# Spreading a head pair's two reciprocal sums over columns: one DVE copy of a broadcast view in place of two ACT operations

## The reference

```python
score = einsum('bqh,bqhs->bqs', wb, relu(einsum('bqhd,bsd->bqhs', qib, k_idx)))
_, idx = lax.top_k(where(causal, score, -inf), 256)      # the keys each query may see
att = einsum('bqhd,bqkd->bhqk', qb, k[idx]) * HEAD_DIM ** -0.5 - slopes * dist
p = jax.nn.softmax(att, axis=-1)                         # 8 query heads, one key/value head
y = einsum('bhqk,bqkd->bqhd', p, v[idx])                 # HEAD_DIM = 64
```

## Time and profile before

| | |
|---|---|
| median of 3 runs | 3352.51 us (3343.8 to 3353.59) |
| the profiled execution, its own time | 3356.66 us |
| its span | 3354.5 us |
| PE busy | 3200.5 us, 95% |
| DVE busy | 2065.4 us, 62% |
| ACT busy | 1310.3 us, 39% |
| POOL busy | 743.8 us, 22% |
| mean granted clock of TensorE | 0.981 of full speed |

### The profile page before, as it was taken

How to read it: one execution, slowest core, us unless ns; L and a number is a source line. 1 busy time by engine, 2 the same in 40 slices (tenths; PEclk the granted TensorE clock), 3 DMA queues, 4 the chain that set the end, 5 groups by cost and what they waited for, 6 DMA issues and landing times.

```text
span 3354.5 us, 41929 instructions
## 1 busy us (share of the span) xinstructions
PE 3200.5 (95%) x15077; PEld 2640.3 (79%) x15077; DVE 2065.4 (62%) x3529; ACT 1310.3 (39%) x2277; POOL 743.8 (22%) x546
## 2 busy tenths in 40 slices
PE   8987999999999999999999999999899998989998
PEld 7865788788888788778887778876788887778886
DVE  5997457688808448598994853759868288610001
ACT  4336421533238431441113843137773177421111
POOL 3431200065774000011322400000211323001212
PEclk9998999999999999999999999999999999999999
DMA  7973756599992656535554055652455510445554
GB/s 228 304 239 122 290 191 207 182 288 291 289 297 108 245 202 218 182 145 195 190 199 145 20 220 203 219 199 81 163 191 198 195 51 20 171 150 193 196 189 169
DMA packets 178528, 635.97 MB, mean 190 GB/s; under 512 B 11357, under 2 KB 96905, under 8 KB 116776
## 3 DMA queue, kind: packets, MB, share of 16 engines
q1 hardware_dynamic: 163728, 582.00, 50.2%
q10 hardware_dynamic: 14616, 51.47, 3.9%
HBM read 474.04 MB, written 159.38 MB: 189 GB/s over the span
## 4 chain that ended last, share of the span: by engine, by line
PE 75%; DVE 7%; ACT 4%; issue 4%; DMA 1%; POOL 0%; ACTq 0%; DVEq 0%; POOLq 0%; SPq 0%
PE PS L1763 19%; PE PS L1725 14%; PE PS L1727 14%; PE PS L1726 14%; PE PS L1930 3%; PE PS L1748 1%; PE PS L1749 1%; PE PS L1750 1%; DVE probs L1593 1%; PE PS L1949 1%; PE PS L1950 1%; PE PS L1809 1%; ACT TMP L838 1%; ACT probs L958 1%; PE PS L1977 1%
## 5 line engine op out<-in xcount | busy, mean ns | idle before, releaser
L1763 PE MATMUL PS<-WS,HT 128*128 128x512 f32 x2088 | 484.3, 392 | 16.1 <-ACT TMP L1082 10.4
L1763 PEld LDWEIGHTS PS<-WS,HT 128*128 128x128 f32 x2088 | 394.5, 189 | 99.7 <-ACT TMP L1082 10.8
L553 POOL TENSOR_TENSOR WS<-RAW,WS 128x1024 fp32r<-128x1024 f32 x116 | 281.1, 2424 | 577.5 <-ACT WS L709 562.2
L1725 PE MATMUL PS<-HF,WS 128*128 128x512 f32 x1024 | 400.5, 391 | 6.9 <-DVE HF L1171 4.6
L637 POOL TENSOR_TENSOR TMP<-TMP 128x512 f32<-128x512 f32 x88 | 113.6, 1291 | 1316.2 <-ACT TMP L1082 1316.2
L1726 PE MATMUL PS<-HF,WS 128*128 128x512 f32 x1024 | 400.1, 391 | 0.0
L1727 PE MATMUL PS<-HF,WS 128*128 128x512 f32 x1024 | 400.0, 391 | 0.0
L1351 DVE TENSOR_SCALAR_CACHE_REDUCE flags<-W,cand 128x640 uint8<-128x640 f32 (+9 forms) x272 | 372.6, 1370 | 35.6 <-DVE cand L1386 27.8
L1725 PE MATMUL PS<-HT,WS 128*128 128x512 f32 x816 | 322.2, 395 | 0.8 <-POOL WS L553 0.6
L1727 PE MATMUL PS<-HT,WS 128*128 128x512 f32 x816 | 317.7, 389 | 0.0
L1726 PE MATMUL PS<-HT,WS 128*128 128x512 f32 x816 | 317.6, 389 | 0.0
(11 more groups left out here) (283 smaller groups left out, 6490.0 us busy)
## 6 DMA issues: line engine op xcount, KB each, us to landing
WS<-split_weights_scratch SPq DMA_DIRECT2D x234, 1024.0 KB, 4.8
split_weights_scratch<-WS SPq DMA_DIRECT2D x116, 1024.0 KB, 5.0
W<-split_weights_scratch SPq DMA_DIRECT2D x114, 1024.0 KB, 4.8
RAW<-in_w_in SPq DMA_DIRECT2D x34, 512.0 KB, 6.0
RAW<-in_w_ffn_gate SPq DMA_DIRECT2D x22, 512.0 KB, 6.3
RAW<-in_w_ffn_up SPq DMA_DIRECT2D x22, 512.0 KB, 6.4
RAW<-in_w_ffn_down SPq DMA_DIRECT2D x22, 512.0 KB, 5.7
gate_b_scratch<-TMP ACTq DMA_DIRECT2D x32, 256.0 KB, 5.3
```

What stands on the lines that cost most here:

```text
L553: nc.gpsimd.tensor_tensor(out=WS[:, slot, 1, :], in0=RAW[:, slot, :], in1=WS[:, slot, 0, :].bitcast(f32), op=ALU.subtract).then_inc(w_lo, 1)
L1725: mm(PS[:, bank, :], wh, src[:, 0, k, :], start=k == 0, stop=False)
L1763: ins = mm(PS[:, 2 * t + half, :], lhs, split(c, w_part)[:, half * 512:(half + 1) * 512], start=first and part == 0 and w_part == 0, stop= ...
```

## The change

DVE takes over the spreading. Behind its reciprocal it waits for its own result and copies a broadcast view of `rs` (each of the two values read 64 times) to the 128 columns of `rsb`, in one operation. ACT's `spread_sums` and its two calls are gone, and so is the tile `ones`, with the memset of POOL that filled it at the start. DVE's wait ahead of the reciprocal is now for `pv_psum` (PE has read the place of `rsb` that is to be written) and no longer for ACT's spreading of two pairs before; PE waits for one count of `rsb_ready` a pair instead of two, and, from the third pair on, also for `bc_done` of two pairs before.

```diff
-                    def spread_sums(n):
-                        act.wait_ge(recip_done, n + 1)
-                        if n >= 2:
-                            act.wait_ge(pv_psum, n - 1)
-                        for f in range(2):
-                            nc.scalar.activation(rsb[:, n % 2, DH * f:DH * f + DH], ones[:, :], ACT.Copy,
-                                                 scale=rs[:, n % 2, f:f + 1]).then_inc(rsb_ready, 1)
...
-                                if e == 1 and u == 0:
-                                    spread_sums(PAIRS * g + i - lag)
...
-                            if i >= lag and e == 1 and not banks:
-                                spread_sums(PAIRS * g + i - lag)
...
                                     if n >= 2:
-                                        dve.wait_ge(rsb_ready, 2 * n - 2)
+                                        dve.wait_ge(pv_psum, n - 1)
...
                                     nc.vector.reciprocal(rs[:, n % 2, :], total).then_inc(recip_done, 1)
+                                    dve.wait_ge(recip_done, n + 1)
+                                    nc.vector.tensor_copy(rsb[:, n % 2, :].rearrange("p (f d) -> p f d", f=2),
+                                                          rs[:, n % 2, :].rearrange("p (f o) -> p f o", o=1).to_broadcast([P, 2, DH])).then_inc(rsb_ready, 1)
...
-                            pe.wait_ge(rsb_ready, 2 * n + 2)
+                            pe.wait_ge(rsb_ready, n + 1)
+                            if n >= 2:
+                                pe.wait_ge(bc_done, n - 1)
```

More of the change, by code:

```diff
@@ L240, in build_block @@
         meanm = sb("meanm", [P, P], f32)
-        ones = sb("ones", [P, DH], f32)
         upper = sb("upper", [P, P], f32)
@@ L563, in _ @@
             nc.gpsimd.memset(meanm[:, :], 1.0 / CC)
-            nc.gpsimd.memset(ones[:, :], 1.0)
             chained(nc.gpsimd.memset(upper[:, :], 0.0))
```

## The result

The changed kernel takes 3364.11 us (median of 5 runs, 3361.67 to 3369.03), the kernel before beside it 3352.14 (median of 5). By these medians it is 12.0 us slower. The recorded ratio, which is not that of the two medians (1.0036), is 1.0048 with a 95% interval of 1.0036 to 1.0059, that is 16 us, 12 to 20. Forecast were 3369.1 us and +14.5. Of the 5.0 us between forecast and median, 2.5 are the size of the change, the rest is the base I counted from (3354.6 against 3352.14). One of the 11 executions of the version in which POOL's product waits for the copy took 12777 us at a mean granted clock of 0.55, and its ratio is of the ten others.

What follows compares the result with a forecast made beforehand. Mostly TensorE bounds the kernel, but in attention groups 0 and 2 a loop of engine waits. Groups 0 to 3 added 6.4, 2.0, 4.4 and 1.7 us, together 14.5, on 3354.6: 3369.1 us, range 3354 to 3389.

Steps and rivals of the forecast that it cites:

- What bounds the loop: Attention groups 0 and 2: engines wait in a loop, and DVE's part from reciprocal to exponential lies on it; turn 3.44 us.
- The step of one copy: Behind DVE's reciprocal: 0.26 us a pair, 0.49 where POOL's product holds the copy in group 0, 0.28 in group 2.
- Rival 3: All groups: copy takes one column a cycle and doesn't meet POOL; step 0.34 us, 13.2 us in all, 3367.8 us; chance 8%.
- Group 0: First attention stage: 13 pairs at 0.49 us, 2 at 0.26, less half a microsecond: +6.4 us.
- ACT's relief: ACT's two spreading operations gone: nothing in groups 0 and 2, -1.5 us in group 1, -1.4 in group 3.
- Group 1: Second attention stage, PE full: copies 1.3 us, a meeting with POOL 2.2, less 1.5 for ACT: +2.0 us.
- the meeting with POOL's 2.40 us product: Group 1, one pair: POOL's product with the gain begins just ahead of the copy and holds it, 2.2 us.
- Group 2: Third attention stage: 16 pairs at a step of 0.28 us make 4.5, of which 4.4 us were taken.
- Group 3: Fourth attention stage: step on the loop at 12 of 16 pairs, 3.1 us, less 1.4 for ACT: +1.7 us.
- the copy that was to find POOL idle: Group 3, four pairs: POOL's product already holds DVE's sum, so the copy behind it meets no POOL work.
- rival 1: POOL's scaling by a scalar per partition holds the copy too, mainly four pairs of group 3; 28 us, 3382.6 us; chance 33%.
- Rival 4: Group 2: POOL's next operation takes the port ahead of the waiting copy in 8 pairs; 21 us more, 3390 us; chance 4%.

Runs made afterwards that it cites:

- the repetition: The changed kernel run and profiled once more, unchanged, on the second chip: 3361.08 us, ratio 1.0031 to the kernel before.
- the second trace of before: Groups 0 to 2, unchanged there, in the profile of the kernel before with one POOL wait added in group 3 alone; that kernel took 3338.41 us.
- the kernel with both spreadings: The kernel before, ACT's spreading kept and used, plus DVE's copy behind the reciprocal into a place nobody reads: 3364.29 us, ratio 1.0043.

## Why the prediction was right, and where its sizes were not

**What bounds the loop.** Right. DVE's part between reciprocal and exponential is the pace in most turns of groups 0 and 2: the copy there costs its step, behind two or three maskings it costs little, and without ACT's spreading nine of the 15 turns of group 0 stay. The pair of the earlier trace rows alone couldn't tell: DVE's result and the end of ACT's spreading come within 0.05 us of each other there. The other six turns had ACT on the loop as well.

**The step of one copy.** Right in all its parts, with 13 held copies in group 0 as counted: 0.04 for the wait, 0.23 for the copy (0.22 taken), 0.49 where POOL's product holds it, 0.26 to 0.33 in group 2 (0.23 at the first pair). The rule of the Trainium skill on the copy through both ports (Vector Engine (DVE) Microarchitecture Reference, 5.1 Performance modes) agrees: the broadcast view cost nothing that shows, 226 ns against 215 ns for the plain copy of 120 columns. Rival 3 falls.

**Group 0, mis-sized.** The term 13 x 0.49 + 2 x 0.26 - 0.5 = 6.4 measured 4.2 us, and 4.3 between the repetition and the second trace of before. The steps of DVE are there, but I took all 15 turns to be the same loop from two of them. Five of the 15 kept their length within 0.01 us, though three of them begin with a held copy: in the one from 298.42 PE was busy for 3.56 of 4.00 us at the half clock, and the rest are turns whose end waits for another engine. Ten turns lengthened, by 0.42 on average. ACT's relief, put at nothing, is worth 1.1 us by itself but 0.1 beside the copy, so that part held.

**Group 1, wrong in sign.** +2.0 was forecast, -1.2 measured. 0.7 of the 1.2 is the clock of the first turn; at a clock of 1.00 in both it is -0.5. Taken apart at that clock, DVE's copies cost 0.65 us (1.3 were charged) and the relief beside them gives 1.2 (1.5 were taken), as the kernel with both spreadings shows. What failed is the third part: the meeting with POOL's 2.40 us product at one pair, 2.2 us, didn't take place. POOL came to it later against the reciprocal: its small product began 0.02 ahead of the reciprocal's start (1078.93 against 1078.95), where it had been 0.33 (1074.58 against 1074.91). So the product with the gain began at 1079.34, behind the copy's start at 1079.14, where it had begun 0.08 ahead of the reciprocal's end. The copy took 0.33 us. One other copy of the group met the end of that product and was held for 0.4 us (0.64 instead of 0.23), which I hadn't counted. A meeting with a margin of 0.08 us can't be carried over to a schedule that the change itself moves by 0.26 a pair; I should have taken it at a chance.

**Group 2, right in its step.** 16 x 0.28 = 4.4 was forecast and 5.5 measured. Of the first 14 turns 12 are longer, by 0.26 to 0.35 each, and two keep their length within 0.1, 3.7 us in all; the last is longer by 1.8. In that, after an idle of 1.12 us, PE ran at a clock of 0.67 over 5 us (1957 to 1962). The kernel with both spreadings has the copies and the same idle but keeps a clock of 1.00 there; its last turn is 0.3 us longer than before, and the group comes to 4.3 us. So 1.5 us of the 5.5 are the clock, in both traces of the changed kernel. This I hadn't counted, and what decides at which clock PE goes on there no run tells.

**Group 3, mis-sized.** +1.7 was forecast, +4.4 and +3.8 measured. The step that failed is the copy that was to find POOL idle: at four pairs POOL's scaling holds it, 0.76 us long and not 0.23. That is rival 1, but not at its price of 2.5. Without the scaling group 3 is at +0.75 (181.47 against 180.72), 3.1 less, 2.0 of it by the turns with these copies and 0.9 by the clock of one turn. So the forecast was wrong that the copy finds POOL idle, and rival 1, that it is held to POOL's end, was wrong as well. The rule of the Trainium skill (SBUF — State Buffer, Who interferes with whom), that GpSimd holds the ports for a whole instruction, fits the two-input products here to 0.1 us; for the scaling of 1024 columns (2.85 and 2.77 us) the traces contradict it, since copy and sum are free 1.0 to 1.2 us behind its start.

**Rival 4** falls by the row of group 2: the copy that waits goes ahead of POOL's next operation, as in the row at 874.41.

**The sum.** The errors, -2.2, -3.2, +1.1 and +2.7, nearly cancel (in the first trace), which is luck, and some of what they cancel is the clock. The sign and the mechanism rest on groups 0 and 2 and don't depend on it. What I had before me and didn't use: the earlier trace rows showed a stall of 2.3 us four times in the kernel before, nearly as much as the whole change costs, and the earlier trace rows the half clock behind one; one wait of POOL removes both.

Open are two things. Why POOL's scaling of 1024 columns stops holding DVE after 1.0 to 1.2 us of its 2.8 isn't settled; nor is what bounds each of the turns that kept their length in group 0, but for the one shown.

## What to carry to other kernels

An operation moved to an engine with a lower busy share is not cheaper if it lands between two engines that wait for each other: in group 2 a copy of DVE cost 0.3 us a turn right behind the reciprocal and at most 0.1 behind three maskings, while DVE is busy for 83 and 84% of that stage. Beside such a change look for what DVE and POOL hold of each other: ask of each short operation of DVE inside SBUF what POOL began just ahead of it, and let POOL's long two-input one start behind it. Compare single stages only between traces whose clock is the same there. And take a meeting of two engines with a margin smaller than the shift that the change brings as a chance, not as a term.

## What was not expected of the hardware

POOL's scaling of 1024 columns (one input) held DVE for a part of its time only: 1.19 us with a scalar per partition, 1.05 with a constant, of 2.85 and 2.77. A copy that began later under it was recorded as long, but delayed nothing. This one, of group 1, is recorded until 0.08 behind the end of L582 (1065.12), while the masking behind it starts 0.15 after the copy's start, as behind a free copy:

```profile
1062.26 2.86 POOL L582 TENSOR_SCALAR attn<-attn,ssq 128x1024 f32<-128x1024 f32 x1
...
1064.11 1.09 DVE L1607 COPY attn<-rs 128x128 f32<-128x128 f32 x1
1064.26 1.08 DVE L1578 CUSTOM_DVE_ANT_0 probs<-PS,QI 128x896 f32<-128x896 f32 x1
```

With the scalar per partition, a sum of DVE that began 0.05 us behind the scaling passed in 0.15 us; with the constant, one that began 0.07 behind it was held for 0.98. What the length of the copy's record means in the group 1 row, and why the sum passes beside the one form and not beside the other, no run here tells.
